# Fox attention in a two-layer encoder kernel: gate sums spread by transfers, scores of two heads side by side, sums of squares in two rounded passes, ones by memset

## The reference, cut to what matters

```python
q = rms_norm(a_q.reshape(bsz, L, FOX_HEADS, FOX_HEAD_DIM), fox_q_gain[l])
k = rms_norm(a_k.reshape(bsz, L, FOX_HEADS, FOX_HEAD_DIM), fox_k_gain[l])
c = jnp.cumsum(jax.nn.log_sigmoid(f_logit), axis=1)
s = jnp.einsum('bhqd,bhkd->bhqk', q, k) * scale + c[q rows] - c[k columns]
p = softmax(where(mask, s, -inf));  out = p @ v
```

## Time and profile before

| | |
|---|---|
| median of 3 runs | 1018.65 us (1017.72 to 1018.83) |
| profiled execution | 1019.28 us |
| its span, first to last instruction | 1017.5 us |
| PE busy | 1008.7 us, 99% |
| DVE busy | 734.4 us, 72% |
| ACT busy | 559.8 us, 55% |
| POOL busy | 225.8 us, 22% |
| granted clock of PE | 1.000 |
| moved by transfers | 178.38 MB, 175 GB/s |

### The profile page before, as it was taken

The page is one execution under the profiler, slowest core; times in us unless marked ns, Lnnn a source line. Parts: engine busy times, 40 slices in busy tenths (PEclk is TensorE's granted clock), DMA queues, the critical chain, the costliest instruction groups (busy, mean ns, idle before and its releaser), DMA issues.

```text
span 1017.5 us, 20399 instructions
## 1 busy us (share of the span) xinstructions
PE 1008.7 (99%) x8434; PEld 941.5 (93%) x8434; DVE 734.4 (72%) x937; ACT 559.8 (55%) x701; POOL 225.8 (22%) x293
## 2 busy tenths in 40 slices
PE   9999999999999999999999999999999999999998
PEld 8898989999999989898999898999999998989898
DVE  5777777889788666666667777777988867565654
ACT  5747453556587645353576555356566865444441
POOL 0004999610002000000020079994000020000000
PEclk9999999999999999999999999999999999999999
DMA  8654545434235454545465454544332355554541
GB/s 304 237 197 164 207 165 206 167 125 147 106 125 207 166 209 164 206 165 206 167 219 213 145 227 150 221 154 174 135 144 104 112 220 190 184 201 170 197 174 42
DMA packets 26817, 178.38 MB, mean 175 GB/s; under 512 B 3120, under 2 KB 4160, under 8 KB 5760
## 3 DMA queue, kind: packets, MB, share of 16 engines
q1 hardware_dynamic: 25056, 172.50, 46.3%
q10 hardware_dynamic: 1584, 4.57, 1.2%
q0 software_dynamic: 112, 0.40, 0.1%
HBM read 176.42 MB, written 1.05 MB: 174 GB/s over the span
## 4 chain that ended last, share of the span: by engine, by line
PE 92%; DVE 3%; DMA 2%; ACT 2%; issue 1%; SPq 0%; POOL 0%; DVEq 0%; ACTq 0%
PE ps L917 24%; PE ps L855 17%; PE ps L856 16%; PE ps L857 16%; PE ps L919 12%; DMA raw<-stream 1%; ACT hi L600 1%; DVE lo L1271 1%; DMA mask<-masks 1%; PE ps L1027 1%; PE ps L1132 1%; DVE in_lo L1490 0%; PE ps L1076 0%; PE ps L1098 0%; SPq L385 0%
## 5 line engine op out<-in xcount | busy, mean ns | idle before, releaser
L917 PE MATMUL ps<-xg,hi 128*128 128x512 f32 x1120 | 397.8, 399 | 0.3
L1271 DVE TENSOR_TENSOR lo<-raw,hi 128x2048 fp32r<-128x2048 f32 x129 | 301.2, 2362 | 132.8 <-ACT hi L600 132.8
L919 PE MATMUL ps<-xg,lo 128*128 128x256 f32 x1120 | 314.5, 281 | 0.0
L600 ACT ACTIVATE hi<-raw 128x2048 fp32r<-128x2048 f32 x129 | 242.6, 1911 | 108.9 <-PE ps L919 81.8
L917 PEld LDWEIGHTS ps<-xg,hi 128*128 128x128 f32 x1120 | 210.5, 188 | 52.0 <-DVE lo L1271 0.9
L919 PEld LDWEIGHTS ps<-xg,lo 128*128 128x128 f32 x1120 | 211.7, 189 | 0.0
L855 PE MATMUL ps<-act_hi,hi 128*128 128x256 f32 x704 | 199.3, 283 | 1.1 <-DVE act_lo L1323 1.1
L856 PE MATMUL ps<-act_lo,hi 128*128 128x256 f32 x704 | 199.2, 283 | 0.0
L857 PE MATMUL ps<-act_hi,lo 128*128 128x256 f32 x704 | 199.1, 283 | 0.0
L855 PEld LDWEIGHTS ps<-act_hi,hi 128*128 128x128 f32 x704 | 134.8, 191 | 3.1 <-issue 1.2
L857 PEld LDWEIGHTS ps<-act_hi,lo 128*128 128x128 f32 x704 | 135.0, 192 | 0.0
(11 more groups left out here) (329 smaller groups left out, 1701.6 us busy)
## 6 DMA issues: line engine op xcount, KB each, us to landing
raw<-stream SPq DMA_DIRECT2D x160, 1024.0 KB, 4.9
par<-params ACTq DMA_DIRECT2D x2, 1463.0 KB, 7.6
raw<-stream SPq DMA_DIRECT2D x8, 256.0 KB, 6.9
rows<-stream SPq DMA_DIRECT2D x2, 1024.0 KB, 7.0
x<-xT ACTq DMA_DIRECT2D x4, 256.0 KB, 6.2
out<-x SPq DMA_DIRECT2D x4, 128.0 KB, 1.9
out<-x ACTq DMA_DIRECT2D x4, 128.0 KB, 2.0
con<-consts POOLq DMA_DIRECT2D x1, 373.5 KB, 6.3
```

Source lines behind the costliest of these rows:

```text
L600: e.activation(hi[slot][:, :], raw[slot][:, :], ACT.Copy).then_inc(hi_written, 1)
L917: pe.matmul(bank(b), hi[slot][:, w:w + P], xg[:, k, :, :].rearrange("p s t -> p (s t)"), start=k == 0, stop=False, skip_group_check=True)
L919: last = pe.matmul(bank(b)[:, 0:T], lo[slot][:, w:w + P], xg_hi[:, k, :], start=False, stop=k == KT - 1, skip_group_check=True)
L1271: v.tensor_tensor(lo[slot][:, :], raw[slot][:, :], hi[slot][:, :].bitcast(F32), ALU.subtract).then_inc(lo_written, 1)
```

## The change

It does six things.

- `ones` is no longer loaded: POOL sets it with a memset at the start. Con comes in two transfers around it, mask in a third. ACT and the row sums wait for the memset; DVE's `angles`, PE's `lag_matrix` and POOL's new step wait for the three transfers.
- The running sum is taken of the negated log gates. SP stores its four rows to a DRAM buffer `cum_rows` and, when that has landed, reads them back spread over all 128 partitions into `gate_bias` (two transfers). This stands in SP's program ahead of the load of unit 8.
- POOL adds the causal mask to `gate_bias` (two additions of 128x512); `fox_mask` adds `gate_bias` to the scores in place of the mask. The term of the query row is dropped.
- DVE no longer writes the six gate rows, POOL no longer clears fqk. fqk is half as large: two heads lie on partitions 0 to 63 and 64 to 127, `fox_scores` multiplies 64 rows for each, and `normalize` is two instructions of 128x512.
- The sums of squares use rounded operands: ACT rounds `halves` and the squares (`fsq_hi`), DVE writes the rest (`fsq_lo`, `low_squares`), PE does two matmuls of 512 columns in place of one in f32. `low_squares(0)` stands between the split of unit 8 and the S5 product, `low_squares(1)` between scores(2) and extend(3).
- The two parameter columns for the gate rows go.

```diff
@@ SP, in the loop over the mixer's loads
                 for w in range(IN_UNITS):
+                    if w == RING + 5:
+                        sp.wait_ge(cum_ready, l + 1)
+                        sp.dma_start(cum_rows, fl[0:FOX_HEADS, 2, :]).then_inc(cum_stored, 16)
+                        sp.wait_ge(bu_done, l + 1)
+                        sp.wait_ge(cum_stored, l * 16 + 16)
+                        for at, n in ((0, P), (P, T)):
+                            sp.dma_start(gate_bias[:, :, at:at + n],
+                                         cum_rows[:, 0:n].unsqueeze(0).broadcast_to([P, FOX_HEADS, n])
+                                         ).then_inc(cum_spread, 16)
@@ POOL, start
+            pool.memset(ones, 1.0).then_inc(ones_set, 1)
             pool.wait_ge(raw_loaded[2], 16)
-            pool.dma_start(con[:, :], consts).then_inc(consts_loaded, 16)
+            pool.dma_start(con[:, 0:P], consts[:, 0:P]).then_inc(consts_loaded, 16)
+            pool.dma_start(con[:, 2 * P:], consts[:, 2 * P:]).then_inc(consts_loaded, 16)
@@ POOL, layer
-                pool.memset(fqk[0:64, :, 1:FOX_HEADS:2, :], 0.0).then_inc(heads_cleared, 1)
                 pool.memset(attn[:, :, :], 0.0).then_inc(attn_cleared, 1)
+                pool.wait_ge(consts_loaded, 48)
+                pool.wait_ge(cum_spread, (l + 1) * 32)
+                causal = cmask[:, P:].unsqueeze(1).broadcast_to([P, FOX_HEADS, P])
+                for at in (T, 0):
+                    block = gate_bias[:, :, at:at + P]
+                    pool.tensor_tensor(block, block, causal, ALU.add).then_inc(bias_ready, 1)
@@ ACT, start; the row sums of PE have the same edit
-            e.wait_ge(consts_loaded, 32)
+            e.wait_ge(ones_set, 1)
@@ ACT, fox_norm
+                    if w == 0:
+                        e.activation(halves_r[:, :], halves, ACT.Copy).then_inc(halves_rounded, 1)
+                    e.wait_ge(fsq_ready, l * 2 + w + 1)
+                    e.activation(fsq_hi[:, w, :], fsq[:, w, :], ACT.Copy).then_inc(fsq_hi_ready, 1)
@@ PE, fox_sums
-                    pe.matmul(bank(6 + w), halves, fsq[:, w, :], start=True, stop=True).then_inc(fsum_done, 1)
+                    pe.matmul(bank(6 + w), halves_r[:, :], fsq_hi[:, w, :], start=True, stop=False)
+                    pe.matmul(bank(6 + w), halves_r[:, :], fsq_lo[:, w, :], start=False, stop=True).then_inc(fsum_done, 1)
@@ PE, fox_scores
-                    for hd in (2 * pair, 2 * pair + 1):
-                        r = slice(0, GATES if hd % 2 == 0 else P)
-                        last = pe.matmul(bank(6 + hd % 2)[:, pair * n:(pair + 1) * n], fqk[r, 0, hd, tok],
-                                         fqk[r, 1, hd, 0:n], start=True, stop=True, skip_group_check=True)
+                    for odd in range(2):
+                        r = slice(64 * odd, 64 * odd + 64)
+                        last = pe.matmul(bank(6 + odd)[:, pair * n:(pair + 1) * n], fqk[r, 0, pair, tok],
+                                         fqk[r, 1, pair, 0:n], start=True, stop=True, skip_group_check=True)
@@ DVE, after the running sum
-                cum = fl[:, 2, :]
-                v.wait_ge(heads_cleared, l + 1)
-                for odd in range(2):
-                    r = slice(0, 2 * FOX_HEADS) if odd else slice(64, GATES)
-                    v.tensor_scalar(fqk[r, 0, odd:FOX_HEADS:2, :], ...)
-                    for hd in (odd, odd + 2):
-                        last = v.tensor_scalar(fqk[r, 1, hd, :], cum[r, :], ...)
-                last.then_inc(cum_ready, 1)
...
+                def low_squares(w):
+                    v.wait_ge(fsq_hi_ready, l * 2 + w + 1)
+                    v.tensor_tensor(fsq_lo[:, w, :], fsq[:, w, :], fsq_hi[:, w, :].bitcast(F32), ALU.subtract
+                                    ).then_inc(fsq_lo_ready, 1)
+
                 take(6, plain[:, 1, :, :])
                 split_in(4)
+                low_squares(0)
...
                 scores(2)
+                low_squares(1)
                 extend(3)
@@ DVE, normalize
-                    for odd in range(2):
-                        r = slice(64 * odd, 64 * odd + 64)
-                        last = v.scalar_tensor_tensor(fqk[r, w, odd:FOX_HEADS:2, :], plain[r, w, :, :], gain[r, :],
-                                                      fsq[r, w, :].rearrange("p (a t) -> p a t", a=2),
-                                                      ALU.mult, ALU.mult)
-                    last.then_inc(fqk_ready, 1)
+                    v.scalar_tensor_tensor(fqk[:, w, :, :], plain[:, w, :, :], gain,
+                                           fsq[:, w, :].rearrange("p (a t) -> p a t", a=2),
+                                           ALU.mult, ALU.mult).then_inc(fqk_ready, 1)
@@ DVE, fox_mask
+                    v.wait_ge(bias_ready, l * 2 + 2 - t)
-                                               cmask[:, 2 * P - n:].unsqueeze(1).broadcast_to([P, 2, n]), ALU.add)
+                                               gate_bias[:, odd:4:2, at:at + n], ALU.add)
```

More of the change, by code:

```diff
@@ L194, in build @@
         fox_mem = ExitStack()
-        fqk = sb("fqk", [P, 2, FOX_HEADS, T], F32, fox_mem)
+        fqk = sb("fqk", [P, 2, 2, T], F32, fox_mem)
+        with ExitStack() as rounded:
+            fsq_hi = sb("fsq_hi", [P, 2, 2 * T], F32R, rounded)
+            halves_r = sb("halves_r", [P, P], F32R, rounded)
+            sb("over_halves", [P, 512 - P], F32, rounded)
+            fsq_lo = sb("fsq_lo", [P, 2, 2 * T], F32R, rounded)
+        sb("over_fqk", [P, 4 * T], F32, fox_mem)
         fv = sb("fv", [P, 2, 256], F32, fox_mem)
@@ L215, in build @@
         pT = w_lag[:, :, :, :].rearrange("p a b c -> p (a b c)")
+        gate_bias = pT.rearrange("p (h c) -> p h c", c=384)
+        cum_rows = nc.dram_tensor("cum_rows", (FOX_HEADS, T), F32, kind="Internal").ap()
         fst = sb("fst", [P, 4, 8])
@@ L329, in build @@
         fsq_ready = sem("fsq_ready")
+        fsq_hi_ready = sem("fsq_hi_ready")
+        fsq_lo_ready = sem("fsq_lo_ready")
+        halves_rounded = sem("halves_rounded")
         fsum_done = sem("fsum_done")
@@ L340, in build @@
         cum_ready = sem("cum_ready")
-        heads_cleared = sem("heads_cleared")
+        cum_stored = sem("cum_stored")
+        cum_spread = sem("cum_spread")
+        bias_ready = sem("bias_ready")
         sc_done = sem("sc_done")
@@ L1080, in fox_sums @@
                 def fox_sums(w):
-                    pe.wait_ge(fsq_ready, l * 2 + w + 1)
+                    pe.wait_ge(fsq_lo_ready, l * 2 + w + 1)
+                    pe.wait_ge(halves_rounded, l + 1)
                     if w == 0:
@@ L1637, in _ @@
                 st.wait()
-                st.mark(v.tensor_tensor(fl[:, 0, :], fl[:, 0, :], fl[:, 1, :], ALU.subtract))
+                st.mark(v.tensor_tensor(fl[:, 0, :], fl[:, 1, :], fl[:, 0, :], ALU.subtract))
                 st.wait()
-                st.mark(v.tensor_tensor_scan(fl[:, 2, :], ones[0:GATES, 0:1].broadcast_to([GATES, T]), fl[:, 0, :], 0.0,
-                                             ALU.mult, ALU.add))
+                v.tensor_tensor_scan(fl[:, 2, :], ones[0:GATES, 0:1].broadcast_to([GATES, T]), fl[:, 0, :], 0.0,
+                                     ALU.mult, ALU.add).then_inc(cum_ready, 1)
                 st.mark(v.tensor_scalar(fst[:, 0, 0:1], prm("q_gain"), FOX_DIM ** -0.5, None, ALU.mult))
                 st.wait()
-                cum = fl[:, 2, :]
-                v.wait_ge(heads_cleared, l + 1)
-                for odd in range(2):
-                    r = slice(0, 2 * FOX_HEADS) if odd else slice(64, GATES)
-                    v.tensor_scalar(fqk[r, 0, odd:FOX_HEADS:2, :], cum[r, :].unsqueeze(1).broadcast_to([2 * FOX_HEADS, 2, T]),
-                                    prm("query_rows", 0, 1)[r, :], prm("query_rows", 1, 1)[r, :], ALU.mult, ALU.add)
-                    for hd in (odd, odd + 2):
-                        last = v.tensor_scalar(fqk[r, 1, hd, :], cum[r, :], prm("key_rows", 2 * hd, 1)[r, :],
-                                               prm("key_rows", 2 * hd + 1, 1)[r, :], ALU.mult, ALU.add)
-                last.then_inc(cum_ready, 1)
                 take(5, plain[:, 0, :, :])
@@ L1840, in _params @@
     rows = np.r_[0:2 * FOX_HEADS, 64:GATES]
-    bias, query, key = np.zeros((GATES, 1)), np.zeros((GATES, 2)), np.zeros((GATES, FOX_HEADS, 2))
+    bias = np.zeros((GATES, 1))
     bias[rows, 0] = np.tile(inputs["fox_f_bias"][l], 4)
-    for r in (0, 64):
-        query[r:r + FOX_HEADS, 0] = query[r + FOX_HEADS:r + 2 * FOX_HEADS, 1] = 1.0
-        for hd in range(FOX_HEADS):
-            key[r + hd, hd, 1], key[r + FOX_HEADS + hd, hd, 0] = 1.0, -1.0
     put("f_bias", bias)
-    put("query_rows", query)
-    put("key_rows", key.reshape(GATES, -1))
     forget = inputs["w_in"][l][:, 3 * 256:3 * 256 + FOX_HEADS]
```

11 lines of the change are left out of this document (6 added, 5 removed).

## The result

The change made the kernel slower: 1022.97 us (median of 7, 1020.1 to 1024.51) against 1017.89 (median of 7), a ratio of 1.0043 with an interval of 1.0033 to 1.0052. I had forecast 1017.6 and a range up to 1021.2. The profiled execution took 1020.75 us, 1.47 more than the one before, with a span of 1019.0 and a granted clock of 0.998 in place of 1.000. Two of the seven stand at a clock of 0.998, two at 0.997, and three at 0.995 with 1023.9 to 1024.5.

A forecast was written before the change was run, and what follows sets the result against it. PE, busy 99% of the span, was taken to bound the kernel. Start -1.25 and two layers of +0.1 (0.6 + 0.5 - 0.78 - 0.3 + 0.1) gave -1.0: 1018.3 profiled, 1017.6 us median, range 1014.6 to 1021.2.

The forecast's parts named there:

- The load of unit 8: Layer, first half: load issued behind store and two spreads, so DVE gets it late; +0.5 us a layer (0 to 2).
- Start, -1.25: Kernel start: ones by memset lets ACT's splits and act_lo come earlier; gain 1.25 us (ends 0.86 and 2.7).
- low_squares(0), +0.6: DVE chain into level(3): one more 128x512 subtraction between in_lo and the S5 product; loss 0.6 us a layer.
- Rival B: Spread slow, unit 8 late: 2 us or more lost a layer, 1020.6 us (1022.6 at 3 us); chance 0.16.
- Sums, -0.78 a layer: Layer's sums of squares: two rounded matmuls replace each f32 one of 0.86 us; gain 0.78 us a layer.
- Normalize, -0.3: Layer's normalize: two 128x512 steps replace four 64x512, removing PE's wait before the scores; gain 0.3 us a layer.
- Scores side by side, +0.1: Layer's 64-row score matmuls: overlap, but each block pays a toll of 0.37 us; loss 0.1 us a layer.
- A (no toll): Rival on the scores: part-array form nearly free on rows, -1.3 a layer, 1014.8 us; chance 0.22.
- D (no overlap): Rival on the scores: pairs don't overlap by rows, +1.4 us a layer, 1020.4 us; chance 0.06.
- POOL's additions: Layer: two 128x512 additions fall in DVE's idle ahead of take(6); if later they meet in_lo, within unit 8's 2 us.

The follow-up runs named there:

- before_spread: Kernel before plus only SP's store and spreads ahead of unit 8's load and POOL's two additions, result unused: 1022.28 us, ratio 1.0036.
- start_only: Kernel before with the start's edits alone (ones by memset, con in two transfers, waits moved to its readers): 1017.75 us, ratio 0.9996.
- late_spread: Changed kernel with SP's store and the two spreads ahead of the load of unit 11 instead of unit 8: 1018.69 us, ratio 1.0006.
- late_dve: Changed kernel with store and spreads behind unit 8's load and the two mask additions on DVE after scores(4), not POOL: 1016.45 us, ratio 0.9991.
- stall4: Kernel before with four extra DVE additions of 128x512 ahead of extend(2), result overwritten: 1027.75 us, ratio 1.0087.
- stall2: Kernel before with two extra DVE additions of 128x512 ahead of extend(2), result overwritten: 1021.62 us, ratio 1.0036.
- mended: late_dve with low_squares(0) moved after scores(2) and low_squares(1) after scores(3): 1017.61 us, ratio 0.999.
- late_spread_low: late_spread with low_squares(0) also moved behind scores(2), beside low_squares(1): 1020.18 us, ratio 1.0017.
- pool_queue: Changed kernel with the store and both spreads issued by POOL in its own queue, and low_squares(0) behind scores(2): 1022.24 us, ratio 1.0034.
- wide_scores: Changed kernel with each score matmul over all 128 rows, which sums two heads: 1022.24 us, ratio 1.0036.

## Why the prediction was wrong

**The step that failed is "The load of unit 8", mis-sized at +0.5 us, and with it the sum, which had no term for the clock.** In the profiled execution the two close the account: I summed to 1018.3 and it took 1020.75, 2.45 more; unit 8 held DVE up for 0.87 + 1.62 = 2.49 us in place of 1.0, which is 1.5 more, and the clock cost 0.9. The other 2.2 us, from there to the median of 1022.97, lie in executions without a trace. Their clocks (0.997 and 0.995) point to two and three falls, and one was seen to cost 0.9 to 1.5 us, so by this estimate one or two more falls make 1 to 3 us. So in the median execution the clock probably weighs more than unit 8's 1.5; that is argued, not shown. By its own steps:

- *Start, -1.25:* right in mechanism: -1.26 between the row sums, with ACT starting at the landing I gave (24.27 for 24.4) and PE at 33.90 for 34.0. That the size fits so well is partly luck. The start that I took it from was a slow one: in before_spread, whose start is that of before, the mask landed by 21.14 instead of 23.82, and PE reached the first mixer's row sums at 205.37, earlier than the changed kernel did (206.42). In medians start_only shows 0.9 without the falls. And PE came to act_lo at 31.38, not 32.55, so it waited 2.52 us and not 1.3; the prediction gave that wait no price of its own, but behind it the clock fell in four of start_only's eleven executions.
- *low_squares(0), +0.6:* right. The wait of 0.79 in late_spread and late_dve is 0.2 + 0.6, and goes to 0.17 when it is moved.
- *Load of unit 8, +0.5 (0 to 2):* the mechanism was right, the size wrong. Everything here ran 1.3 us earlier, by the start's gain (the scan ended at 244.72 instead of 246.04), and DVE needed the unit that much earlier too; so the landing at 254.78 stands for 256.1 beside my 255.75. From the end of the scan I had 2.8 us to the load's issue and 6.9 from there to its landing. In layer 1 the store was faster (1.3 us to the spreads instead of 2.0), but issuing the two spreads took 2.0 us instead of 0.8: 3.3 to the issue, then 6.73. In layer 2 the load was issued 2.3 us after the scan, but took 8.95. I had taken the spreads as bytes at 418 GB/s with something on top; they took 3.8 and 5.8 us to landing themselves. Why the load behind them took 6.73 once and 8.95 the other time is not shown. DVE stood 0.87 and 1.62 us for it, of which none was there before. My terms gave a wait for the key of 0.2 + 0.6 + 0.5 = 1.3 a layer; it was 1.74 and 2.49. Rival B had this mechanism at 2 us or more a layer, more than either; that the median lies beyond its 1020.6 is not by its mechanism alone.
- *The missing term:* around the end of a wait of 2.49 us in layer 2 the granted clock went to half, which cost 0.9 us. Of its seven executions the after kernel has none at 1.000 and three at 0.995. stall4 shows the price by itself: 9.3 us of time for 5.8 us of added waiting, against 3.2 for 2.9 in stall2.
- *Sums, -0.78 a layer:* right. The two matmuls take 0.47 us, and from level(3) to level(7) the mended kernel takes 11.36 us in layer 2, 0.78 less than the 12.14 before.
- *Normalize, -0.3:* the wait is gone; the rest is too small to tell.
- *Scores side by side, +0.1:* right in mechanism, a little low. Four matmuls of 64x256 (two of the kernel, two records each) and their neighbours:

```profile
273.87 0.28 PE L893 MATMUL ps<-in_hi,h_lo 128*128 128x256 f32 x1
274.08 0.70 PE L1170 MATMUL ps<-fqk 64*128 64x256 f32 x4
...
274.94 0.28 PE L892 MATMUL ps<-in_lo,h_hi 128*128 128x256 f32 x1
```

  One more matmul (at 274.71, left out) streams for 0.12 ahead of the last row, so the block took (274.94 - 0.12) - (273.87 + 0.12) = 0.83, against 0.80 forecast. The blocks of 64x128 took 0.62 in the same way, against 0.58; together +0.26 a layer for my +0.1. Halved streams (0.43 and 0.22) leave a toll of 0.40 a block. Rivals A (no toll) and D (no overlap) are out. The Trainium skill's drain on a change of tiling mode ("TensorEngine Tiling (Array Packing)", Key Properties) agrees with this toll of 0.40 us, though no run separates the drain from other costs of such a block.
- *POOL's additions:* in the change they fell into DVE's idle, as forecast (252.39 to 254.9). I said they would cost if they came later; late_spread shows 0.7 to 0.9 us a layer for that. The Trainium skill, "SBUF — State Buffer", Who interferes with whom, says that VectorE and GpSimd share one pair of ports, and one waits while the other holds it; the rows here agree, at 1.54 and 1.77 us for steps of 0.69.

How the causes add up in medians: the change +5.1; with the transfers behind unit 8, +0.5 (a difference of 4.6 us for cause 1 and the falls behind it, the largest share, less what the additions then cost by meeting DVE); with the additions in DVE's idle, -1.5; with a start that waits less and the squares moved, -2.9. The medians of before differ by 0.6 us between chips, so the last digit is not to be trusted.

A list of PE's longer waits in the profiles, and the clock behind each, shows how far wait and fall belong together:

| wait of PE, us | where | clock in the next windows |
|---|---|---|
| 1.07 | before, act_lo | 1.00 |
| 1.50 | late_dve, act_lo | 1.00 |
| 1.67, 1.68 | stall2, key, both layers | 1.00; 1.00 |
| 1.74 | after, key, layer 1 | 1.00 |
| 1.78 | late_spread_low, act_lo | 1.00 |
| 1.82 | late_spread_low, key, layer 2 | 0.69, 0.50 |
| 1.93 | start_only, act_lo | 0.50, 0.70 |
| 1.9 | before_spread, key, layer 2 | 0.65, 0.50 |
| 1.94 | pool_queue, act_lo | 0.71, 0.50 |
| 2.0 | wide_scores, key, layer 1 | 0.50, 0.66 |
| 2.07 | mended, act_lo | 0.58, 0.57 |
| 2.25 | pool_queue, key, layer 1 | 0.50, 0.76 |
| 2.49 | after, key, layer 2 | 0.50, 0.91 |
| 2.50 | wide_scores, act_lo | 1.00, 1.00 |
| 2.52 | after, act_lo | 1.00, 1.00 |
| 3.1 | stall4, key, both layers | 0.50, 0.77; 0.50, 0.50 |

The waits of 1.3 to 1.7 us that are not listed had no fall behind them either. The rows at 2.50 and 2.52 keep it from being a rule: a long wait does not always bring the fall. What else decides stays open.

## What to carry to other kernels

Where PE is busy 99% of the span, price a new wait of PE not by its length alone: ask what the granted clock does behind it, since behind a wait of about 2 us a fall cost 0.9 to 1.5 us more, in some executions only. A gain that makes PE arrive earlier at the same late producer turns work into waiting; move the producer too (here the order of ACT and DVE at the start, on top of the memset, was worth more than the memset alone). Read a gain at the start from several executions, since the profiled one may have had a slow start. And ahead of a load that somebody needs soon, a transfer counts by its own measured time to landing and by what it adds to the load's, not by its bytes; behind that load it was nearly free.

## What the runs showed that I had not expected

- A memset in place of a transfer left the median where it was (0.9996), by splitting the executions into two kinds 1.7 us apart.
- A 1 MB load behind two spreads (256 and 512 KB in runs of 512 and 1024 bytes) took 6.73 and 8.95 us to landing, against 4.9.
- The same spreads issued by POOL took 4.9 and 7.4 us to landing, and kept its additions waiting 8.13 us in layer 1 and 5.39 in layer 2.
- The start of before, unchanged, differs by 2.3 us between profiles (first mixer's row sums at 205.37 to 207.68).
- PE gaps of 0.55 to 1.1 us with no releaser, in layer 1 of three kernels whose key was on time, and not in two others.
